# A hybrid decoder layer on one core: rotation one chunk later, extra products in the norm stage, attention scores as three split products

## The reference, cut to what matters

```python
xn = rmsnorm(x, g) * (1 + sc) + sh                 # sc, sh from silu(c) @ w_ada
qa, ka, va, qb, fb, ib, ogb, ga, gb = split(xn @ w_in)
q, k = rope(rmsnorm(qa)), rope(rmsnorm(ka))        # 8 heads x 2 halves x 64
p = softmax(causal(q0 k0 / 8)) - lam * softmax(causal(q1 k1 / 8))
oa = rmsnorm(p @ va)                               # differential attention
ob = rmsnorm(hgrn2(silu(qb), 1 - f, log f, ib)) * silu(ogb)   # gated recurrence, state 128 x 128
x = x + g_m * ((sigmoid(ga) * (oa @ w_a) + sigmoid(gb) * (ob @ w_b)) @ w_out)
x = x + g_f * (conv_ffn(modulated rmsnorm(x)))
```

## Time and profile before

| | us |
|---|---|
| median of 3 runs | 2242.23 (2240.45 to 2244.01) |
| the profiled execution | 2243.18 |
| its span, first to last instruction | 2241.4 |
| PE busy | 2210.7 (99%) |
| PE weight loads busy | 2100.9 (94%) |
| DVE busy | 1557.2 (69%) |
| ACT busy | 1175.5 (52%) |
| POOL busy | 939.0 (42%) |

### The profile page before, as it was taken

How to read it: one execution, slowest core, us unless ns; L and a number is a source line. 1 busy time by engine, 2 the same in 40 slices (tenths; PEclk the granted TensorE clock), 3 DMA queues, 4 the chain that set the end, 5 groups by cost and what they waited for, 6 DMA issues and landing times. The chain is left out here.

```text
span 2241.4 us, 47969 instructions
## 1 busy us (share of the span) xinstructions
PE 2210.7 (99%) x18881; PEld 2100.9 (94%) x18881; DVE 1557.2 (69%) x2574; ACT 1175.5 (52%) x2449; POOL 939.0 (42%) x1144
## 2 busy tenths in 40 slices
PE   7999999999999999999999999999999999999999
PEld 5899998989999989989988999999999999999999
DVE  5668687877778686876677515417988888876545
ACT  6567665766666666665444511114566666643110
POOL 1135262634444352626322224442165665635431
PEclk9999999999999999999999999999999999999999
DMA  8212122231213121222789623112344555485212
GB/s 310 86 55 94 46 86 67 59 105 56 99 50 105 44 88 56 70 89 88 273 301 367 244 44 121 48 48 93 123 179 185 188 186 185 175 317 190 86 48 95
DMA packets 103514, 288.35 MB, mean 129 GB/s; under 512 B 18426, under 2 KB 26490, under 8 KB 103290
## 3 DMA queue, kind: packets, MB, share of 16 engines
q1 hardware_dynamic: 102138, 281.09, 35.4%
q10 hardware_dynamic: 1152, 4.19, 0.5%
HBM read 213.18 MB, written 63.77 MB: 124 GB/s over the span
## 5 line engine op out<-in xcount | busy, mean ns | idle before, releaser
L172 PE MATMUL ps<-xn_hi,h_w_hi 128*128 128x344 f32 x1680 | 549.6, 327 | 2.2 <-PEq L205 0.9
L172 PE MATMUL ps<-xn_hi,h_w_lo 128*128 128x344 f32 x1680 | 536.5, 319 | 0.0
L172 PE MATMUL ps<-xn_lo,h_w_hi 128*128 128x344 f32 x1680 | 536.3, 319 | 0.0
L172 PEld LDWEIGHTS ps<-xn_hi,h_w_hi 128*128 128x128 f32 x1680 | 316.9, 189 | 35.2 <-issue 26.0
L172 PEld LDWEIGHTS ps<-xn_lo,h_w_hi 128*128 128x128 f32 x1680 | 315.6, 188 | 0.7
L172 PEld LDWEIGHTS ps<-xn_hi,h_w_lo 128*128 128x128 f32 x1680 | 315.7, 188 | 0.0
L1247 POOL TENSOR_TENSOR h_w_lo<-h_w_raw,h_w_hi 128x1024 fp32r<-128x1024 f32 x58 | 149.2, 2573 | 384.2 <-ACT h_w_hi L809 348.9
L3188 DVE SCALAR_TENSOR_TENSOR x<-ps,keep_mod,x 128x344 f32<-128x344 f32 x168 | 94.3, 570 | 163.3 <-PE ps L3025 100.7
L3025 PE MATMUL ps<-f_act_lo,f_d_hi 128*128 128x344 f32 x528 | 169.4, 321 | 0.0
L3025 PE MATMUL ps<-f_act_hi,f_d_lo 128*128 128x344 f32 x528 | 168.8, 320 | 0.0
L3025 PE MATMUL ps<-f_act_hi,f_d_hi 128*128 128x344 f32 x528 | 168.5, 319 | 0.1
(11 more groups left out here) (468 smaller groups left out, 6556.6 us busy)
## 6 DMA issues: line engine op xcount, KB each, us to landing
h_w_raw<-in_w_in SPq DMA_DIRECT2D x72, 512.0 KB, 3.6
y_rows<-f_y SPq DMA_DIRECT2D x44, 516.0 KB, 2.6
f_y_pair<-y_rows SPq DMA_DIRECT2D x22, 1032.0 KB, 5.4
h_d_ada_w<-in_w_ada SPq DMA_DIRECT2D x32, 512.0 KB, 4.4
g_vp<-in_cache_v SPq DMA_DIRECT2D x32, 512.0 KB, 6.2
f_a<-in_w_ffn SPq DMA_DIRECT2D x57, 256.0 KB, 2.6
g_kp<-in_cache_k SPq DMA_DIRECT2D x28, 512.0 KB, 7.7
h_w_raw<-in_w_mix SPq DMA_DIRECT2D x24, 512.0 KB, 3.5
```

What stands on the lines that cost most here:

```text
L172: ins = eng.matmul(out, w[:, k * P:(k + 1) * P], x[:, k, columns], start=(k == 0 and n == 0), stop=(k == n_k - 1 and n == 2))
```

## The change

1. `keep_clock`: 15 products of 128 x 128 x 128 whose result nobody reads are put between the modulation products of the norm stage.
2. Rotation: DVE does `rope` of piece u in chunk u + 1 and `rope_end` in chunk u + 2 (each one chunk later), in the order `rope_end`, `rope`, `squares_low`. PE makes the sums of squares three k-steps inside the piece, no longer in front of it.
3. Scores: `qT` and `kT` are split into high parts (ACT) and low parts (POOL; DVE at head 0), and each score product becomes three `float32r` products. The high parts lie where the modulation weights of the heads stage lie, so SP loads those only behind the last scores; the low part of q overwrites `qT`, that of k lies in `LQ[0]`.
4. The sums of the attention output's squares go to PSUM banks 2 and 3 of `SP_`; the first scores of the next head wait for their readers.
5. POOL waits for `weighed` before its squares and its weight splits in attention, its squares of `oraw` wait for `sq_low` and no longer for a rotated piece, and `maxima` scales the row maximum with a `tensor_tensor` for a `tensor_scalar`.

```diff
+            def keep_clock(count):
+
+                for _ in range(count):
+                    pe.matmul(G[:, 0, 0:P], mean[:, :], mean[:, :], start=True, stop=True)
...
             ada(0)
+            keep_clock(2)
             ada(1)
             pe.wait_ge(pick_ready.sem, 1)
             pick(0)
+            keep_clock(2)
             ada(2)
+            keep_clock(1)
             pick(1)
+            keep_clock(3)
             pe.wait_ge(lnd.sem, NP)
             for k in range(KT):
                 if k + 3 < KT:
                     ada(k + 3)
+                if k == 0:
+                    keep_clock(1)
                 if k + 2 < KT:
                     pick(k + 2)
+                if k == 0:
+                    keep_clock(6)
...
+NQK = 2 * NP
 KEYS_AT = (3, 4, 5, 7)
+PARTS_AT = (5, 7)
...
+        q_hi, k_hi = part("q_high", parts_at), part("k_high", parts_at + KT * P * 4)
+        q_lo, k_lo, first_k_lo = part("q_low", q_at), part("k_low", lq_at), part("first_k_low", ibtok_at)
...
-            return u % 2 if u < 2 or h == H - 1 else 1
+            if u < 2:
+                return SP_[:, 2 + u, :]
+            return X[:, u % 2 if h == H - 1 else 1, :]
...
-                    if t == 3:
+                    if t == NTL + 1:
+                        sp.wait_ge(scores.sem, scores.at(h, NB))
                         load_ada(h, 0, 0)
...
+            def first_high(j):
+
+                act.wait_ge(qk_ready.sem, 2 * j + 2)
+                for src, hi in ((qT, q_hi), (kT, k_hi)):
+                    act.activation(hi[:, prompt(j)], src[:, prompt(j)], ACT.Copy).then_inc(qk_high.sem, 1)
+
+            def key_high(h, j):
...
+                act.wait_ge(qk_ready.sem, qk_ready.at(h, NP + j + 1))
+                act.activation(k_hi[:, prompt(j)], kT[:, prompt(j)], ACT.Copy).then_inc(qk_high.sem, 1)
...
+                    if k == PARTS_AT[0] and not no_next(h):
+                        act.wait_ge(qk_ready.sem, qk_ready.at(h, NP))
+                        act.activation(q_hi[:, :], qT[:, 0:T], ACT.Copy).then_inc(qk_high.sem, 1)
+                    if k == PARTS_AT[1] and not no_next(h):
+                        key_high(h, 0)
+                        key_high(h, 1)
                     if k == SUMS_AT:
                         o_norm(h, 0)
                         o_norm(h, 1)
+                    if k == PARTS_AT[1] and not no_next(h):
+                        key_high(h, 2)
...
                 nk = (i + 1) * P
-                for m in range(2):
-                    rows = slice(DH * m, DH * (m + 1))
-                    for b in range(0, nk, 512):
-                        w = min(512, nk - b)
-                        ins = pe.matmul(SP_[:, score_bank(i, m) + b // 512, 0:w], qT[rows, i * P:(i + 1) * P], kT[rows, b:b + w],
-                                        start=True, stop=True)
+                j = (nk - 1) // TH
+                pe.wait_ge(qk_low.sem, qk_low.at(h, 2 * j + 2))
+                products = ((q_hi, k_hi), (q_hi, k_lo if h else first_k_lo), (q_lo, k_hi))
+                for b in range(0, nk, 512):
+                    w = min(512, nk - b)
+                    for n, (q, key) in enumerate(products):
+                        for m in range(2):
+                            rows = slice(DH * m, DH * (m + 1))
+                            ins = pe.matmul(SP_[:, score_bank(i, m) + b // 512, 0:w], q[rows, i * P:(i + 1) * P], key[rows, b:b + w],
+                                            start=(n == 0), stop=(n == 2))
                 ins.then_inc(scores.sem, 1)
...
             def attention_sums(h):
                 if no_next(h):
                     pe.wait_ge(rows_ready.sem, 1)
-                else:
-                    pe.wait_ge(qk_ready.sem, qk_ready.at(h, 6))
+                pe.wait_ge(lv_k.sem, lv_k.at(h, NB))
...
                 pe.wait_ge(qk_ready.sem, qk_ready.at(h, 0))
+                if h:
+                    pe.wait_ge(o_rstd.sem, o_rstd.at(h - 1, 2))
...
+                    def piece_sums(u):
+
+                        pe.wait_ge(sq_high.sem, sq_high.at(h, u + 1))
+                        pe.wait_ge(sq_low.sem, sq_low.at(h, u + 1))
+                        if u >= 2:
+                            pe.wait_ge(qk_ready.sem, qk_ready.at(h, u - 1))
+                        qk_sums(u % 2)
+
+                    between = (SUMS_BEHIND, attention_sums, h) if k == SUMS_AT else None
                     if 0 < k <= 6 and not no_next(h):
-                        pe.wait_ge(sq_high.sem, sq_high.at(h, k))
-                        pe.wait_ge(sq_low.sem, sq_low.at(h, k))
-                        if k >= 3:
-                            pe.wait_ge(qk_ready.sem, qk_ready.at(h, k - 2))
-                        qk_sums((k - 1) % 2)
+                        between = (SUMS_BEHIND, piece_sums, k - 1)
                     for n in REC_PIECES[k]:
-                        piece(h, n, (SUMS_BEHIND, attention_sums, h) if k == SUMS_AT else None)
+                        piece(h, n, between)
...
             for h in range(H):
+                pool.wait_ge(weighed.sem, weighed.at(h, 1))
...
+                        if n in SPLIT_AT:
+                            pool.wait_ge(weighed.sem, weighed.at(h, i + 1))
...
-                            pool.wait_ge(qk_ready.sem, qk_ready.at(h, 5))
+                            pool.wait_ge(sq_low.sem, sq_low.at(h, NQK))
...
+                    if k == PARTS_AT[1] and not no_next(h):
+                        pool.wait_ge(os_done.sem, os_done.at(h, k))
+                        for j in range(NP):
+                            for src, hi, lo, high in ((qT, q_hi, q_lo, 1), (kT, k_hi, k_lo, j + 2)):
+                                pool.wait_ge(qk_high.sem, qk_high.at(h + 1, high))
+                                pool.tensor_tensor(lo[:, prompt(j)], src[:, prompt(j)], hi[:, prompt(j)].bitcast(F32), ALU.subtract).then_inc(qk_low.sem, 1)
...
+            def first_low(j):
+
+                for n, (src, hi, lo) in enumerate(((qT, q_hi, q_lo), (kT, k_hi, first_k_lo))):
+                    dve.wait_ge(qk_high.sem, 2 * j + n + 1)
+                    dve.tensor_tensor(lo[:, prompt(j)], src[:, prompt(j)], hi[:, prompt(j)].bitcast(F32), ALU.subtract).then_inc(qk_low.sem, 1)
...
+                if j:
+                    first_low(j - 1)
                 for u in (2 * j, 2 * j + 1):
                     dve.wait_ge(qk_rstd.sem, u + 1)
                     rope_end(j, first_bank[u], first_cos[u], kT if u % 2 else qT)
+            first_low(NP - 1)
...
-                dve.tensor_scalar(sm[:, 2:4], sm[:, 0:2], -SCALE, None, ALU.mult).then_inc(row_max.sem, 1)
+                dve.tensor_tensor(sm[:, 2:4], sm[:, 0:2], sm[:, 8:10], ALU.mult).then_inc(row_max.sem, 1)
...
-                    if k < 6 and not no_next(h):
-                        u, j = k, k % NP
-                        if k:
-                            squares_low(h, k)
-                        dve.wait_ge(qk_cos.sem, qk_cos.at(h, u + 1))
-                        dve.wait_ge(qk_turned[u].sem, qk_turned[u].at(h, 4))
-                        rope(j, rg[u % 3][:, :], rt[u % 2][:, :])
-                    if 0 < k <= 6 and not no_next(h):
-                        u = k - 1
+                    if 0 <= k - 2 < NQK and not no_next(h):
+                        u = k - 2
                         dve.wait_ge(qk_rstd.sem, qk_rstd.at(h, u + 1))
                         if u == 0:
                             dve.wait_ge(sample_qkv.sem, sample_qkv.at(h, 1))
                             dve.wait_ge(kv_stored.sem, kv_stored.at(h, 2))
                         rope_end(u % NP, X[:, u % 2, 0:TH], rg[u % 3][:, :], qT if u < 3 else kT)
+                    if k == 7:
+                        o_norm(h, 0)
+                        o_norm(h, 1)
+                    if 0 <= k - 1 < NQK and not no_next(h):
+                        u = k - 1
+                        dve.wait_ge(qk_cos.sem, qk_cos.at(h, u + 1))
+                        dve.wait_ge(qk_turned[u].sem, qk_turned[u].at(h, 4))
+                        rope(u % NP, rg[u % 3][:, :], rt[u % 2][:, :])
+                    if 0 < k < NQK and not no_next(h):
+                        squares_low(h, k)
```

More of the change, by code:

```diff
@@ L542, in heads_stage @@
         cos, sin, blk, causal, lmask = (early[n] for n in ("cos", "sin", "blk", "causal", "lmask"))
+        q_at = mem.off
         qT, kT, vT = (mem(n, [P, NT]) for n in ("qT", "kT", "vT"))
@@ L546, in heads_stage @@
         kk, fc, qh, ib, og = (mem(n, [P, NT]) for n in ("kk", "fc", "qh", "ib", "og"))
+        ibtok_at = mem.off
         ibtok = mem("ibtok", [P, T])
@@ L553, in heads_stage @@
         LK = [mem(f"LK{i}", [P, LEVELS, P]) for i in range(2)]
+        lq_at = mem.off
         LQ = [mem(f"LQ{i}", [P, LEVELS + 1, P]) for i in range(2)]
@@ L569, in heads_stage, with part @@
         oraw = mem("oraw", [P, T])
+        parts_at = mem.off
```

(21 more changed lines are left out.)

3 lines of the change are left out of this document (removed).

## The result

The changed kernel takes 2250.55 us (median of 6 runs, 2249.32 to 2252.22) against 2242.57 for the kernel before (6 runs): a ratio of 1.0033 (95% interval 1.0021 to 1.0044), 8 us slower, outside the range of the prediction and on the other side of it. The profiled span is 2247.5 us for 2241.4; the profiled execution of the changed kernel was the fastest of its six, so the profiles are 6.1 us apart and the medians 8.

A forecast was written before the change was run, and what follows sets the result against it. PE, busy throughout, was taken to bound the kernel. Scores -4.7, rotation -0.1, head 0 +1.9 and norm stage -1.4 summed to -4.3 us on the profiled 2243.18; predicted 2238 us, range 2229 to 2245.

The forecast's parts named there:

- Where I cost nothing: ACT's high parts, POOL's low parts and `weighed` waits, later modulation weight loads, and row maximum scaling were given no cost.
- The ring: Recurrence chunks: ACT's piece read, `assemble`, `operands`, `rope_end` take 6.65 us a round against 6.04 mean chunks; +5.9 us, seven heads.
- Rotation removed: Later rotation removes chunk 2's 0.59 us stall, 4.1 us over seven heads; 6.0 us removed with other waits.
- The further 1.9 for other waits: Half of nine further PE waits, mean 0.42 us, counted as removed by the later rotation: 1.9 us.
- Scores: Attention's score calls: split products take 8.80 us a head against 9.39; -4.7 us over eight heads, -9.7 at the lower end.
- The six narrow products: Score products of 128 columns, taken at four columns' time: 1.28 us; 0.66 from below, bound by weight loads.
- the prediction's lower end: Score calls at 8.18 us a head, with narrow products bound by weight loads; -9.7 us over eight heads.
- Rival B: Score calls: narrow split products run at one column's time, five us less than forecast, 2233 us; chance 0.23.
- F: Score calls: split products' weight loads on half the rows stand bare, 0.107 us each; +31 us, 2269; chance 0.04.
- Head 0 and the norm stage: Head 0's start: four subtractions before the last rotation, +1.9 us; norm stage: clock products keep the clock up, -1.4 us.
- D: Ring tight from chunk 2 (+4.6 us, 2242.5) and POOL's parts late as well, 7 us per microsecond; chance 0.09.

The follow-up runs named there:

- half a split: Changed kernel, but POOL's split in chunk 6 makes 512 of its 1024 columns and leaves out the rest: 2242.56 us, 0.9996 to the kernel before.
- run 2: Changed kernel with DVE's rotation back where it was (`squares_low(k)`, `rope(k)`, `rope_end(k - 1)` in chunk k): 2240.82 us, 0.9989 to the kernel before.
- run 10: As run 5, with the row maximum scaled by `tensor_scalar` again: 2232.44 us, 0.9957 to the kernel before.
- run 9: Changed kernel with four ring slots for the scaled pieces instead of three: 2247.19 us, 1.0017 to the kernel before.
- run 7: Changed kernel without the 15 clock products: 2254.60 us, 1.0045 to the kernel before.
- run 5: As run 2, and POOL's squares wait for `rope_end(4)` as before, not for `squares_low(5)`: 2233.54 us, 0.9952 to the kernel before.
- runs 1: Changed kernel with `rope_end(k - 2)` moved ahead of `assemble(k)` on DVE: 2254.34 us, 1.0051 to the kernel before.
- 6: As run 5, with `rope` of piece 0 in chunk 1 ahead of `squares_low(1)`, no longer in chunk 0: 2238.84 us, 0.9978 to the kernel before.
- run 4: Changed kernel without POOL's waits for `weighed` before its squares and weight splits: 2261.28 us, 1.0081 to the kernel before.

## Why the prediction was wrong

**The step that failed** is the paragraph "Where I cost nothing", and in it that the first two low parts "are there by 574.7, and PE begins head 4 at 576.19". It asked only whether POOL's work would be late for PE. The runs showed that POOL's operations hold DVE, and DVE then holds PE: at the ends of heads (+3.7, gone with half a split) and in attention (+5.4, of which 3.3 went with the same half split, and all of it with the rotation back, run 2). Together 9 us, in a forecast of -4.3, that I had at nothing. I had quoted the rule that tells of it (the Trainium skill, SBUF — State Buffer, Who interferes with whom: two SBUF inputs on DVE contend with a GpSimd operation that reads SBUF) and read the row of 1.30 us, but used both for the form of the row maximum's scaling alone, which makes no difference (run 10); that "PE doesn't wait there" was no longer so, since that scaling, held for 1.67 us, stands in the chain in front of block 3. The moved `rope`, two operations with both inputs in SBUF, went past the 2.4 us split without a price.

**The ring** was seen rightly: 6.65 us worked out, 6.60 measured, and its share was 5.6 us in chunks 3 to 5 (run 9) for the 5.9 predicted. These chunks lose 10.0 us in all. What is left, 4.3, is there with four slots too. In that trace 3.8 of it lie inside the pieces of chunks 3 and 5, where the sums of squares wait for `squares_low`, now the last of DVE's three. I had given them nine products, 1.4 us, more time and so no price. What of the delay comes from POOL's holds and what from the order was not separated, and 2.6 of the 5.6 us came back in chunks 6 and 7.

**Rotation removed:** 4.0 us in chunk 1 for the 4.1 predicted. The further 1.9 for other waits was not found.

**Scores:** the model of the calls held at 512 columns (a last call of 1.60 us, 1.57 predicted). The six narrow products were mis-sized, so the calls gained 1.20 us a head for 0.59: they take 8.18 us, the prediction's lower end. Rival B's mechanism was right, its time not. F is out: two halves of split products on half the rows run side by side with their loads hidden. The Trainium skill's rule (TensorE: Matmul & The Clock Gate, Part 3, The mechanism), by which loads overlap only on other row groups, doesn't describe these calls: 12 products of 512 columns end in 1.60 us. On each half they start 0.23 us apart, where with the prediction's 0.107 us for a bare load they would be 0.32 apart (estimate).

**Head 0 and the norm stage:** +1.5 for +1.9 and -1.2 for -1.4. In the norm stage the clock products are worth more than the comparison with the kernel before shows: 2.4 us (run 7). In head 0 no gain by them is shown.

**The rivals:** D was on the right side with the wrong road. It had the low parts late for PE; the first two of head 4 are there at 578.7, PE begins the head at 580.1, and no wait of PE ended at POOL.

So the change holds a gain and two losses. What is left without the losses, split scores and clock products above all, is 11 us faster than the kernel before (run 5); the rotation one chunk later costs 10 (run 2) and, with the wait that starts POOL's squares earlier, 18 (run 5).

## What to carry to other kernels

When an operation moves on an engine, list what the other engines run at its new time, and price the meeting, not only the dependences: here a DVE operation with both inputs in SBUF waited out all that was left of a POOL operation it had nothing to do with, up to 2.2 us. Ask where a ring of buffers closes when its release moves behind other work, and count that ring in time before any gain. And when a move removes a stall, look for the stretch that has just as little slack right behind it: runs 1, 6 and 9 all pushed the lateness on by one or two chunks.

## What the runs showed of the hardware

- A DVE operation with two tensor inputs, both in SBUF, that starts while a longer POOL operation runs ends behind it, by a time that goes with its own columns. In the profile of the changed kernel that was 0.02 us for 2 columns (L1512, 31 of 31), 0.28 for 256 (L1523, 6 of 6), 0.38 for 344 (L1438, 9 of 9) and 0.55 for 512 (L3423, 50 of 50). So its own size says little of its time: 2.60 us for an addition of 344 columns (0.52 alone), 1.30 us for a product of one column (0.16 alone, run 4). Those with an input in PSUM were not held (L1569, 23 of 23, at 0.35 us). A `tensor_scalar` was held as well (1.15 us for 0.28, run 4). POOL was held the other way round where DVE had started first: 2.68 us for a split of 2.39.
- Split products of 128 columns on 64 rows start 0.06 to 0.17 us apart, two halves together, and of 512 columns 0.23 us, about as on all rows (0.24 in the earlier trace rows).
- Without the small filling products the granted clock was 0.52 on average from 25 to 35.5 us, where it was 1.00 with them. With them it could still fall elsewhere: in run 4 to a mean of 0.83 from 80 to 90 us, where head 0 starts behind a wait of PE, and from 845 to 855 us, behind a wait of 1.60 us.
